# Transposed powers of a chunked scan made on VectorE, and a new order of the second token tile's stages

## Chip, cores and metric

One core of one Trainium2 chip (trn2). The metric is the device time of one execution in microseconds. TensorE's clock has two levels, 1.2 and 2.4 GHz; the profile shows the granted clock as a share of the upper one.

## The reference, cut to what matters

256 tokens of width 1024, all in f32, pass through two blocks. The first mixes the tokens and then retrieves 128 rows for each token out of 16384 (gathered from HBM by index). The second is a hybrid layer with 32 experts:

```
h = rms_norm(x) * (1 + scale1) + shift1
proj = h @ w_in
y_rwkv = rwkv7_time_mix(...)      # per head: state = state * w + (state @ -kk) (kk*a)^T + v k^T
y_moba = moba_attention(...)      # causal attention here, one block of 256 keys
x = x + gate1 * (concat(y_rwkv, y_moba) @ w_out)
h = rms_norm(x) * (1 + scale2) + shift2
x = x + gate2 * moe(h)            # top 4 of 32 experts, each with 12 MB of weights
```

The recurrence of the time mix runs over all 256 tokens, for 8 heads of 64 channels.

## The kernel before

**Two tiles of 128 tokens.** After the first block's mixing, the kernel retrieves 256 picks (128 for each tile): GpSimd gathers a row for each of 128 tokens, VectorE makes the dot products, ScalarE the weights, TensorE the weighted sums. The second block's mixing of the first tile (all of the hybrid layer up to the router) is spread over the retrieval of the second tile's picks; the second tile's mixing follows alone. Then come the 32 experts, each with six 2 MB pairs of weight chunks.

**What sets the order.** Every engine runs the stages of a tile as generators (`attention`, `values`, `mixer`, `output`), which yield a stage's name before it. For the first tile, `first_slots()` gives each name a pick, and an engine runs the stage at that pick (`up_to`; ScalarE one pick ahead, TensorE two). For the second tile, `to_end` always takes the generator whose next stage stands first in the hand-written list `ORDER`. Each engine executes in its order and waits on semaphores; a generator's own order is never changed by the list.

**The scan.** The time mix works in chunks of 32 tokens (`CL`). Per chunk and head, "gram0" and "gram1" are the products of the scaled keys with the scaled queries (L2229, masked by VectorE at L1618). The inverse of a strictly triangular 32x32 matrix is built from powers in five levels: `si[:, :, 0]` holds the power S, `si[:, :, 1]` the inverse so far, and `nts`/`pw_t` in turn the transposed power. Each level has two groups of 32 products, the fifth only one (8 heads by 4 chunks, `within`, L2253; each product gives two matmul and two load records): one makes the next transposed power, which ScalarE copies out of PSUM (L1027), the other the next power and the next term of the inverse, which VectorE copies and adds (L1663, L1665). The first transposed matrix comes from TensorE as "nt" (L2243), masked by VectorE (L1652). Then follow z1 and wu (L2253, L2292: the inverse applied), the chunk products fg (L2310), phi (L1682), the state from chunk to chunk (st: L2336 and L1691), q2 and yp (L2320), ys (L2354) and a group norm (ln2, ln3). "tok0" to "tok3" are four transposed tensors (L2213), "aff" is eight small operations that fold the norm's gain and bias into the gate (L1635, L1640).

**The attention.** mb0 to mb3 are the products for query and key, each in two halves (L2071), mb4 and mb5 those for the values (L2128); msum sums the squares (L2078) that VectorE makes (L1405), mscore the scores (L2090; VectorE L1421 reads them), soft the maxima, exp the exponentials on ScalarE, prob the scaling by VectorE (L1438), mturn the turned probabilities (L2101, copied by ScalarE at L934), att the product with the values (L2111).

**The output projection** is in two parts: om0 to om3 for the attention's half (L2411), or0 to or3 for the scan's half (L2371). Norm, router and the first expert follow.

**The weights' queue.** SyncE issues all loads in order. After the stream of the layer's weights come the experts' pairs into ten places. Pairs 1 to 5 wait for the ring slots of rw, mb and others; the sixth waits for att of the second tile (`pv_mm`), the seventh for yp and fg:

```
elif m == 5:
    sp.wait_ge(pv_mm, TT)
elif m == 6:
    sp.wait_ge(yp_mm, TT)
    sp.wait_ge(fg_mm, 4 * TT)
```

The eighth and ninth wait for or1 and or3 (ring slots of the output projection), the tenth for the router, and each later one for the pair that has been read ten before it.

Of the kernel before, what the change touches and what calls it, by code (L numbers as in the profile page):

```python
# [10 lines left out]
ALU = mybir.AluOpType  # L11
# [47 lines left out]
GRAM_BANK = (2, 0)  # L59
TOK_BANK = {3: 4, 0: 1, 1: 3, 2: 4}  # L60
# [117 lines left out]
def first_slots():  # L178
    at = {"sum": 0, "norm": 1, "gain": 2, "norm1": 3, "xn": 4, "xres": 5, "turn": 6, "msq": 20, "msum": 21, "rms": 22, "qk": 23, "mscore0": 24, "soft0": 26,
# [3 lines left out]
          "tok3": 41, "aff": 42, "gram1": 43, "nt": 44, "tok0": 47, "tok1": 51, "tok2": 55, "z1": 64, "wu": 65, "phi0": 71, "phi1": 72, "q2": 78, "yp": 79,  # L183
# [20 lines left out]
rw5.0 rw5.1 exps mixr kmod rw6.0 rw6.1 rkk rw7.0 bonus rw7.1 mixv gup kk mb0.0 mb0.1 tilde mb1.0 mb1.1 bon gram0 tok3 aff mb2.0 mb2.1 gram1 nt  # L204
mb3.0 mb3.1 msq pow1 tok0 msum rms pow2 tok1 mb4.0 qk pow3 tok2 mscore0 soft0 mb4.1 mscore1 exp0 pow4 soft1 mb5.0 pow5 exp1
mb5.1 prob0 z1 mturn0 prob1 wu mturn1 fg0 fg1 fg2 fg3 att phi0 st0 phi1 om0 st1 om1 st2 q2 yp om2 st3 ys ln2 om3 ln3
# [61 lines left out]
def build(nc, xd, stream, colsd, matsd, rowsd, badad, expert_uv, w_gate_up, w_down, bias_moe, out):  # L268
    with ExitStack() as ctx:
# [261 lines left out]
        nt_mm = sem("nt_mm")  # L531
# [3 lines left out]
        pt_mm = sem("pt_mm")  # L535
# [246 lines left out]
        def _(act):  # L782
# [163 lines left out]
            def mixer(tt):  # L946
# [92 lines left out]
                act.preload_act_table_set("natural_log_exp_and_others")  # L1039
# [74 lines left out]
        def _(dve):  # L1114
# [283 lines left out]
            def attention(tt):  # L1398
# [42 lines left out]
            def mixer(tt):  # L1441
# [180 lines left out]
                grams(0)  # L1622
                yield "tok3"
# [6 lines left out]
                yield "aff"  # L1630

                dve.wait_ge(tilde, tt + 1)
                dve.wait_ge(sig_out, 9 * tt + 9)
                for c in range(4):
                    dve.scalar_tensor_tensor(bon[tt][:, c, :], bon[tt][:, c, :], col("ln_b", c), gg[tt][:, c, :], ALU.add,  # L1635
                                             ALU.mult).then_inc(vec_step, 1)
                steps[0] += 4
                dve.wait_ge(vec_step, steps[0])
                for c in range(4):
                    dve.tensor_scalar(gg[tt][:, c, :], gg[tt][:, c, :], col("ln_g", c), None,  # L1640
                                      ALU.mult).then_inc(vec_step, 1)
                steps[0] += 4
# [993 lines left out]
```

## Time and profile before

| | |
|---|---|
| median of 3 runs | 1935.63 us (1935.39 to 1938.67) |
| the profiled execution | 1940.42 us, span 1938.6 us |
| TensorE, matmuls busy | 1709.2 us, 88% |
| VectorE busy | 918.2 us, 47% |
| ScalarE busy | 471.6 us, 24% |
| GpSimd busy | 285.6 us, 15% |
| HBM read | 770.53 MB, 398 GB/s over the span |
| mean granted clock | 0.942 |

The shares are averages over stages with different limits: mixing of the first block (to about 190 us), retrieval (to about 887 us), the second tile (to about 1016 us) and the experts. The 2 MB pairs of the experts take 28.6 us from issue to landing by the page, because several are on their way at once. A line of the timeline merges successive instructions of one kind, and the idle time in brackets is that before the first of them. "issue" as a releaser means that the engine waited for nothing that the profile shows.

### The profile page before, as it was taken

The page shows a single profiled execution, that of the slowest core. Times are in us where ns is not written, and L with a number is a line of the kernel's source. Part 1 is how long each engine was busy: PE and PEld are TensorE (multiplying, and loading weights), DVE is VectorE, ACT ScalarE, POOL GpSimd, SP SyncE. Part 2 cuts the span into 40 slices and gives each one's busy share as a digit, 9 for nine tenths or more (in the row PEclk, how much of TensorE's full clock was granted, in tenths as well). Part 3 has the DMA queues.
Part 4 walks back from the last instruction along what each step waited for, and adds up shares of the span by engine and source line. Part 5 has one row for each costly group of instructions (what it writes and reads, how often), then busy time and mean ns, then how long its engine had stood idle before and what let it go on. Part 6 is the DMA issues. An engine that isn't in the chain of part 4 may idle for free.

```text
span 1938.6 us, 29728 instructions
## 1 busy us (share of the span) xinstructions
PE 1709.2 (88%) x12010; PEld 801.4 (41%) x12010; DVE 918.2 (47%) x1994; ACT 471.6 (24%) x1191; POOL 285.6 (15%) x286
## 2 busy tenths in 40 slices
PE   9999988666679876879989999999999999999997
PEld 7888554211135533416873333333333333333332
DVE  4755877788664765555532323232323223222222
ACT  1011443433344633443221111011011101111100
POOL 1001433344433243350000000000000000000000
PEclk9999998866679999878999999999999999999999
DMA  9992999999999999999559999999999999999996
GB/s 392 381 410 114 422 420 421 421 421 421 421 421 420 421 419 420 414 414 373 234 219 388 426 427 427 428 428 428 428 428 428 427 428 428 428 428 428 428 428 294
DMA packets 81850, 772.98 MB, mean 399 GB/s; under 512 B 9076, under 2 KB 9332, under 8 KB 10200
## 3 DMA queue, kind: packets, MB, share of 16 engines
q1 hardware_dynamic: 44192, 500.50, 61.5%
q0 software_dynamic: 36864, 268.45, 33.4%
q10 hardware_dynamic: 696, 2.66, 0.4%
q8 instruction: 69, 1.13, 0.2%
q14 instruction: 29, 0.24, 0.0%
HBM read 770.53 MB, written 1.05 MB: 398 GB/s over the span
## 4 chain that ended last, share of the span: by engine, by line
PE 39%; DMA 8%; DVE 4%; issue 2%; ACT 0%; SPq 0%; DVEq 0%; ACTq 0%
PE psum L2476 18%; PE psum L2507 10%; DMA ring<-in_w_gate_up 4%; PE psum L2519 3%; DMA gates_mats<-in_w_gate_up 2%; DMA arena<-in_w_gate_up 2%; PE psum L2172 1%; PE psum L2490 1%; DVE arena L1821 1%; DVE arena L1824 1%; DVE arena L1818 1%; DVE arena L1819 1%; PE psum L2071 1%; PE psum L2462 1%; PE psum L2128 0%
## 5 line engine op out<-in xcount | busy, mean ns | idle before, releaser
L2036 PE MATMUL psum<-ring,arena 64*64 64x512 f32 x1584 | 267.5, 759 | 130.5 <-ACT arena L903 130.1
L1392 DVE CUSTOM_DVE_ANT_0 ring<-ring,arena 128x1024 f32<-128x1024 f32 x198 | 241.7, 1225 | 133.7 <-DMA ring<-in_expert_uv,arena 131.9
L2476 PE MATMUL psum<-ring,arena 128*64 128x512 f32 x1232 | 273.3, 594 | 3.3 <-DMA ring<-in_w_gate_up 3.2
L767 POOL DMA_INDIRECT ring<-in_expert_uv,arena x198 | 211.8, 1070 | 321.4 <-PE psum L2036 299.8
L1818 DVE TENSOR_SCALAR arena<-psum 128x512 f32<-128x512 f32 x32 | 22.1, 692 | 374.3 <-PE psum L2476 374.3
L1102 ACT ACTIVATE arena<-arena 128x512 f32<-128x512 f32 x32 | 20.2, 630 | 732.1 <-DVE arena L1818 732.1
L2036 PEld LDWEIGHTS psum<-ring,arena 64*64 64x64 f32 x1584 | 49.2, 153 | 286.1 <-ACT arena L903 272.3
L2476 PEld LDWEIGHTS psum<-ring,arena 128*64 128x64 f32 x1232 | 86.5, 137 | 183.8 <-issue 174.9
L2476 PE MATMUL psum<-arena 128*64 128x512 f32 x608 | 136.7, 595 | 1.7 <-DMA arena<-in_w_gate_up 0.9
L2507 PE MATMUL psum<-ring,arena 128*64 128x512 f32 x608 | 136.9, 595 | 0.0
L894 ACT ACTIVATE late<-late 128x1 f32<-128x1 f32 x256 | 51.7, 202 | 309.3 <-DVE late L1392 305.8
L1879 PE MATMUL psum<-arena,ring 128*128 128x256 f32 x512 | 111.7, 379 | 0.1
L1827 DVE TENSOR_TENSOR arena<-psum,arena 128x512 f32<-128x512 f32 x32 | 22.1, 692 | 188.4 <-PE psum L2507 188.4
L1879 PEld LDWEIGHTS psum<-arena,ring 128*128 128x128 f32 x512 | 96.9, 190 | 13.7 <-issue 0.4
L767 POOL DMA_INDIRECT arena<-in_expert_uv,arena x58 | 63.6, 1096 | 257.5 <-DVE arena L1355 170.2
L2036 PE MATMUL psum<-arena 64*64 64x512 f32 x464 | 76.0, 735 | 28.0 <-ACT arena L903 27.9
L1830 DVE TENSOR_TENSOR xres<-xres,psum 128x1024 f32<-128x1024 f32 x64 | 75.3, 1218 | 40.8 <-PE psum L2519 40.8
L1392 DVE CUSTOM_DVE_ANT_0 arena<-arena 128x1024 f32<-128x1024 f32 x58 | 70.9, 1225 | 43.6 <-DMA arena<-in_expert_uv,arena 42.9
L903 ACT ACTIVATE arena<-ident,peer_w 128x64 f32<-128x64 f32 x256 | 89.0, 348 | 8.4
L2519 PE MATMUL psum<-arena 64*128 64x512 f32 x256 | 63.6, 611 | 26.9 <-issue 26.9
L2476 PEld LDWEIGHTS psum<-arena 128*64 128x64 f32 x608 | 42.3, 137 | 91.5 <-issue 87.1
L898 ACT ACTIVATE peer_w<-late,peer_g 128x1 f32<-128x1 f32 x256 | 75.4, 294 | 8.9
(381 smaller groups left out, 2038.7 us busy)
## 6 DMA issues: line engine op xcount, KB each, us to landing
ring<-in_w_gate_up SPq DMA_DIRECT2D x77, 2048.0 KB, 28.6
ring<-in_stream SPq DMA_DIRECT2D x91, 1024.0 KB, 11.1
arena<-in_w_gate_up SPq DMA_DIRECT2D x38, 2048.0 KB, 29.2
ring<-in_w_down SPq DMA_DIRECT2D x38, 2048.0 KB, 28.6
arena<-in_w_down SPq DMA_DIRECT2D x20, 2048.0 KB, 28.6
gates_mats<-in_w_gate_up SPq DMA_DIRECT2D x13, 2048.0 KB, 28.1
gates_mats<-in_w_down SPq DMA_DIRECT2D x6, 2048.0 KB, 30.6
ring<-in_expert_uv,arena POOLq DMA_INDIRECT x198, 17.9
```

Of the source, the lines that this page charges most:

```text
L767: pool.indirect_dma_start(rows_of[b].rearrange("p u d -> p (u d)"), None, expert_uv, bass.IndirectOffsetOnAxis(peer_i[:, tt, k:k + 1], 0)) ...
L894: act.activation(one, one, ACT.Gelu).then_inc(weight_step, 1)
L898: act.activation(peer_w[:, 0, c % 4:c % 4 + 1], one, ACT.Copy, scale=peer_g[:, tt, k:k + 1]).then_inc(weight_step, 1)
L903: act.activation(diag[:, c % 4, :], ident2[:], ACT.Copy, scale=peer_w[:, 0, c % 4:c % 4 + 1]).then_inc(diag_ready, 1)
L1392: dve.tensor_tensor_reduce(u, u, h2[tt], 1.0, 0.0, ALU.mult, ALU.add, peer_h[:, tt, k:k + 1]).then_inc(dot_done, 1)
L1818: dve.tensor_scalar(ag, psum[:, 0, :], LIMIT, None, ALU.min).then_inc(gate_ready, 1)
L1830: dve.tensor_tensor(xres[:, tt, :], xres[:, tt, :], psum[:, (6, 3)[tt]:(8, 5)[tt], :].rearrange("p a c -> p (a c)"), ALU.add).then_inc(acc ...
L1879: last = pe.matmul(psum[:, bank, c * T:(c + 1) * T], wide(n)[:, k, c * P:(c + 1) * P], acts[:, k, :], start=(k == 0), stop=(k == KD - 1))
L2036: last = pe.matmul(psum[o:o + 64, 6 * tt + h, :], diag[rows, c % 4, :], rows_of[b][rows, 1, h * 512:(h + 1) * 512], start=(k == 0), stop=( ...
L2476: last = pe.matmul(psum[CAP * h:CAP * h + CAP, gu, :], x, w[:, at:at + 512], start=False, stop=(kt == GU_CHUNKS - 1), skip_group_check=True)
L2507: last = pe.matmul(psum[CAP * h:CAP * h + CAP, 5, :], a_in, w[:, i * D + h * 512:i * D + h * 512 + 512], start=False, stop=(kt == KD - 1), ...
L2519: last = pe.matmul(psum[:, (6, 3)[tt] + h, :], sct[rows, tt, :], ye[rows, :], start=True, stop=True)
```

## The change

- The transposed matrix and the transposed powers come from VectorE, as transposes of 32x32 blocks from SBUF to SBUF (five of 128x256 a tile). "nt" and the four groups of products for transposed powers (levels 1 to 4) go from TensorE, with their copies on ScalarE; level 4 now makes a power and a term at once (64 columns). All powers go to PSUM bank 2.
- tok0, tok1 and tok2 stand after level 3 and level 5, all copied by ScalarE; tok3 stands before gram0 on TensorE.
- "aff" moves from before gram1 to after the first chunk's state.
- "msq" is two stages, each waiting for its own copy.
- `ORDER`: in the second tile the scan's products stand first, the attention's later stages follow the states, and om0 to om3 stand behind ys.
- The second tile drops one load of ScalarE's table at ln2.

```diff
+POW_BANK = 2
...
-    at = {"sum": 0, "norm": 1, "gain": 2, "norm1": 3, "xn": 4, "xres": 5, "turn": 6, "msq": 20, "msum": 21, "rms": 22, "qk": 23, "mscore0": 24, "soft0": 26,
+    at = {"sum": 0, "norm": 1, "gain": 2, "norm1": 3, "xn": 4, "xres": 5, "turn": 6, "msq0": 16, "msq1": 20, "msum": 21, "rms": 22, "qk": 23, "mscore0": 24, "soft0": 26,
-          "tok3": 41, "aff": 42, "gram1": 43, "nt": 44, "tok0": 47, "tok1": 51, "tok2": 55, "z1": 64, "wu": 65, "phi0": 71, "phi1": 72, "q2": 78, "yp": 79,
+          "nt": 41, "tok3": 42, "gram1": 43, "tok0": 55, "tok1": 56, "tok2": 63, "z1": 64, "aff": 75, "wu": 65, "phi0": 71, "phi1": 72, "q2": 78, "yp": 79,
...
-rw5.0 rw5.1 exps mixr kmod rw6.0 rw6.1 rkk rw7.0 bonus rw7.1 mixv gup kk mb0.0 mb0.1 tilde mb1.0 mb1.1 bon gram0 tok3 aff mb2.0 mb2.1 gram1 nt
-mb3.0 mb3.1 msq pow1 tok0 msum rms pow2 tok1 mb4.0 qk pow3 tok2 mscore0 soft0 mb4.1 mscore1 exp0 pow4 soft1 mb5.0 pow5 exp1
-mb5.1 prob0 z1 mturn0 prob1 wu mturn1 fg0 fg1 fg2 fg3 att phi0 st0 phi1 om0 st1 om1 st2 q2 yp om2 st3 ys ln2 om3 ln3
+rw5.0 rw5.1 exps mixr kmod rw6.0 rw6.1 rkk rw7.0 bonus rw7.1 mixv gup kk mb0.0 mb0.1 tilde mb1.0 mb1.1 bon gram0 nt tok3 mb2.0 gram1 pow1 mb2.1 msq0 pow2
+mb3.0 pow3 tok0 tok1 mb3.1 msq1 pow4 msum rms pow5 tok2 mb4.0 z1 qk mb4.1 mscore0 soft0 wu mb5.0 mb5.1 mscore1 exp0 fg0 fg1 soft1 fg2 fg3
+phi0 exp1 phi1 st0 st1 aff st2 q2 prob0 mturn0 prob1 yp mturn1 st3 att ys om0 om1 ln2 om2 om3 ln3
...
-                for lv in range(1, 5):
-                    yield "pow%d" % lv
-                    dst = (nts, pw_t)[lv % 2][tt]
-                    act.wait_ge(pt_mm, 4 * tt + lv)
-                    act.copy(dst, psum[:, 2, 0:T].rearrange("p (h t) -> p h t", h=NH)).then_inc(pt_out, 1)
-                    if lv in (1, 3):
-                        i = lv - 1
-                        yield "tok%d" % i
-                        act.wait_ge(tok_mm, 4 * tt + i + 2)
-                        dst = tok[tt][:, i, :].rearrange("p (h c) -> p h c", h=NH) if i else az[tt][:, :, 0, :]
-                        act.copy(dst, psum[:, TOK_BANK[i], :].rearrange("p (h c) -> p h c", h=NH)).then_inc(tok_ready, 1)
+                for i in range(3):
+                    yield "tok%d" % i
+                    act.wait_ge(tok_mm, 4 * tt + i + 2)
+                    dst = tok[tt][:, i, :].rearrange("p (h c) -> p h c", h=NH) if i else az[tt][:, :, 0, :]
+                    act.copy(dst, psum[:, TOK_BANK[i], :].rearrange("p (h c) -> p h c", h=NH)).then_inc(tok_ready, 1)
...
-                act.preload_act_table_set("natural_log_exp_and_others")
+                if tt == 0:
+                    act.preload_act_table_set("natural_log_exp_and_others")
...
-                yield "msq"
-                dve.wait_ge(mb_out, 3 * tt + 2)
                 for i, src in enumerate((mq[tt], mk[:, :, tt * P:(tt + 1) * P])):
-                    ins = dve.tensor_tensor(msq[tt][:, i, :].rearrange("p (a t) -> p a t", a=4), src, src, ALU.mult)
-                ins.then_inc(msq_ready, 1)
+                    yield "msq%d" % i
+                    dve.wait_ge(mb_out, 3 * tt + i + 1)
+                    dve.tensor_tensor(msq[tt][:, i, :].rearrange("p (a t) -> p a t", a=4), src, src,
+                                      ALU.mult).then_inc(msq_ready, 1)
...
+                yield "nt"
+                dve.wait_ge(gram_out, 2 * tt + 1)
+                dve.transpose(nts[tt], gr[tt][:, 0, :, 0:CL]).then_inc(nt_out, 1)
+                dve.tensor_tensor(si[tt][:, :, 1, :], gr[tt][:, 0, :, 0:CL],
+                                  ident_c[:].unsqueeze(1).to_broadcast([P, NH, CL]), ALU.add).then_inc(nt_out, 1)
...
-                yield "aff"
+                def affine():
...
-                yield "nt"
-                dve.wait_ge(gram_out, 2 * tt + 1)
-                sh = [P, NH, CL]
-                dve.tensor_tensor(si[tt][:, :, 1, :], gr[tt][:, 0, :, 0:CL], ident_c[:].unsqueeze(1).to_broadcast(sh),
-                                  ALU.add).then_inc(nt_out, 1)
-                dve.wait_ge(nt_mm, tt + 1)
-                dve.tensor_tensor(nts[tt].rearrange("p (c b) t -> p b c t", b=2),
-                                  psum[:, 2:4, 0:P].rearrange("p b (c t) -> p b c t", c=4),
-                                  mask_ts[:].unsqueeze(1).unsqueeze(1).to_broadcast([P, 2, 4, CL]),
-                                  ALU.mult).then_inc(nt_out, 1)
 
                 for lv in range(1, 6):
                     yield "pow%d" % lv
                     dve.wait_ge(ps_mm, 5 * tt + lv)
-                    w = 2 * CL if lv in (2, 3) else CL
-                    out = psum[:, 0, 0:NH * w].rearrange("p (h t) -> p h t", h=NH)
-                    if lv < 4:
+                    w = 2 * CL if 1 < lv < 5 else CL
+                    out = psum[:, POW_BANK, 0:NH * w].rearrange("p (h t) -> p h t", h=NH)
+                    if lv < 5:
                         dve.tensor_copy(si[tt][:, :, 0, :], out[:, :, 0:CL]).then_inc(ps_out, 1)
+                        dve.wait_ge(ps_out, 4 * tt + lv)
+                        dve.transpose((nts, pw_t)[lv % 2][tt], si[tt][:, :, 0, :]).then_inc(pt_out, 1)
                     if lv > 1:
                         dve.tensor_tensor(si[tt][:, :, 1, :], si[tt][:, :, 1, :], out[:, :, w - CL:w],
                                           ALU.add).then_inc(ix_out, 1)
-                    if lv == 2:
-                        yield "tok1"
-                        dve.wait_ge(tok_mm, 4 * tt + 3)
-                        dve.tensor_copy(tok[tt][:, 1, :], psum[:, TOK_BANK[1], :]).then_inc(tok_ready, 1)
...
+                    if c == 0:
+                        yield "aff"
+                        affine()
...
+                yield "tok3"
+                pe.wait_ge(ym_ready, 1)
+                pe.wait_ge(tilde, tt + 1)
+                by_token(3, ps[tt][:, 8:12, :])
...
-                yield "nt"
-                pe.wait_ge(gram_out, 2 * tt + 1)
-                for c in range(4):
-                    for ch in range(P // CL):
-                        ts = chunk_rows(ch)
-                        for par in range(2):
-                            rows = slice(HD * par, HD * par + HD)
-                            last = pe.matmul(psum[ts, 2 + par, c * CL:(c + 1) * CL], ar[tt][rows, c, 0, ts], bt[tt][rows, c, ts],
-                                             start=True, stop=True)
-                last.then_inc(nt_mm, 1)
-
                 def within(bank, lhs, rhs, w):
...
-                    s_src = si[tt][:, :, 0, :] if lv > 1 else gr[tt][:, 0, :, 0:CL]
                     t_src = (pw_t, nts)[lv % 2][tt]
                     yield "pow%d" % lv
                     if lv == 1:
                         pe.wait_ge(nt_out, 2 * tt + 2)
-                        pe.wait_ge(gram_out, 2 * tt + 2)
                     else:
                         pe.wait_ge(pt_out, 4 * tt + lv - 1)
-                        pe.wait_ge(ps_out, 3 * tt + min(lv - 1, 3))
-                    if lv < 5:
-                        within(2, s_src, lambda ts, h: t_src[ts, h, :], CL).then_inc(pt_mm, 1)
                     if lv > 2:
                         pe.wait_ge(ix_out, 4 * tt + lv - 2)
-                    within(0, t_src, (begun, both, both, inverse, inverse)[lv - 1],
-                           2 * CL if lv in (2, 3) else CL).then_inc(ps_mm, 1)
-                    if lv < 4:
-                        yield "tok%d" % (lv - 1)
-                        by_token(lv - 1, (ar[tt][:, :, 0, :], bt[tt], kt_[tt])[lv - 1])
+                    within(POW_BANK, t_src, (begun, both, both, both, inverse)[lv - 1],
+                           2 * CL if 1 < lv < 5 else CL).then_inc(ps_mm, 1)
+                    for i in {3: (0, 1), 5: (2,)}.get(lv, ()):
+                        yield "tok%d" % i
+                        pe.wait_ge(gram_out, 2 * tt + 2)
+                        by_token(i, (ar[tt][:, :, 0, :], bt[tt], kt_[tt])[i])
```

## Rows read from the trace of the kernel before

**Rows 1.** Chain of waits: start us, us, what (its part from 1697 us).
```profile
1697.56 39.38 DMA ring<-in_w_gate_up
```

**Rows 2.** Table of stretches; busy us of each engine (instructions), granted clock, DMA share, GB/s.
```profile
400.00:850.00 450.00, 338.18 (x3356) 142.60 (x3356) 298.46 (x653) 196.15 (x599) 182.51 (x169) 0.84 1.01 419
927.90:1003.00 75.10, 66.22 (x1673) 56.62 (x1672) 31.92 (x76) 19.79 (x40) 0.00 (x0) 0.93 0.52 197
952.30:955.70 3.40, 3.40 (x73) 3.06 (x63) 1.35 (x3) 0.37 (x1) 0.00 (x0) 0.50 0.04 14
979.60:986.50 6.90, 6.41 (x98) 5.78 (x99) 1.71 (x3) 0.58 (x1) 0.00 (x0) 0.51 0.19 38
1023.00:1026.20 3.20, 3.20 (x18) 1.15 (x16) 0.51 (x2) 0.00 (x0) 0.00 (x0) 1.00 0.12 51
1029.00:1900.00 871.00, 834.05 (x4120) 291.33 (x4116) 247.67 (x427) 107.14 (x155) 0.00 (x0) 1.00 1.01 428
```

**Rows 3.** Timeline of SP's queue: start us, us, DMA issued (q: queue).
```profile
984.81 0.33 SPq L671 DMA_DIRECT2D arena<-in_w_down  x1
...
1006.79 4.12 SPq L671 DMA_DIRECT2D ring<-in_w_gate_up  x2
...
1026.26 0.33 SPq L671 DMA_DIRECT2D arena<-in_w_down  x1
```

**Rows 4.** Timeline of TensorE: start us, us, line, operation, count [idle before, releaser].
```profile
927.91 7.41 PE L2071 MATMUL psum<-arena,ring 128*128 128x128 f32 x64
...
945.36 1.31 PE L2253 MATMUL psum<-arena 32*32 32x32 f32 x128
...
951.84 2.18 PE L2253 MATMUL psum<-arena 32*32 32x32 f32 x99 [2.05 <-issue]
...
965.81 0.32 PE L2253 MATMUL psum<-arena 32*32 32x32 f32 x13 [1.30 <-issue]
...
970.59 1.10 PE L2253 MATMUL psum<-arena 32*32 32x64 f32 x64
...
980.09 1.07 PE L2310 MATMUL psum<-arena 32*64 32x64 f32 x48 [2.69 <-issue]
...
993.55 1.06 PE L2320 MATMUL psum<-arena 32*64 32x32 f32 x83 [1.11 <-issue]
...
999.54 1.89 PE L2411 MATMUL psum<-ring,arena 128*128 128x256 f32 x8
1003.04 7.17 PE L2371 MATMUL psum<-ring,arena 128*128 128x256 f32 x32 [1.61 <-DVE arena L1711]
```

**Rows 5.** Groups by line, shapes apart, of VectorE, then ScalarE, 927.9 to 1003.04 us.
```profile
L1421 DVE SCALAR_TENSOR_TENSOR arena<-arena,psum 128x256 f32<-128x256 f32 x8 | 2.8, 416 | 0.8 <-PE psum L2090 0.8
...
L1438 DVE TENSOR_SCALAR arena<-arena,gsm 128x256 f32<-128x256 f32 x8 | 2.3, 350 | 0.1
...
L1618 DVE TENSOR_TENSOR arena<-psum,mask_st 128x512 f32<-128x512 f32 x2 | 1.4, 692 | 4.7 <-PE psum L2229 4.7
...
L1663 DVE COPY arena<-psum 128x256 f32<-128x256 f32 x3 | 1.3, 423 | 8.1 <-PE psum L2253 8.1
L1635 DVE SCALAR_TENSOR_TENSOR arena<-arena,cols 128x128 f32<-128x128 f32 x4 | 1.1, 344 | 0.0
L1640 DVE TENSOR_SCALAR arena<-arena,cols 128x128 f32<-128x128 f32 x4 | 0.9, 282 | 0.0
...
L934 ACT COPY arena<-psum 128x1024 f32<-128x1024 f32 x2 | 2.0, 1012 | 3.4 <-PE psum L2101 3.4
...
L914 ACT COPY arena<-psum 128x512 f32<-128x512 f32 x2 | 1.2, 585 | 16.3 <-PE psum L2071 16.3
```

**Rows 6.** DMA view, queues, 927.9 to 1003 us: packets, MB, share.
```profile
q8 instruction: 14, 0.23, 1.3%
```

**Rows 7.** The page, DMA issues: count, us from issue to landing.
```profile
ring<-in_expert_uv,arena POOLq DMA_INDIRECT x198, 17.9
```

More of the change, by code:

```diff
@@ L530, in build @@
         gram_out = sem("gram_out")
-        nt_mm = sem("nt_mm")
         nt_out = sem("nt_out")
@@ L534, in build @@
         ps_out = sem("ps_out")
-        pt_mm = sem("pt_mm")
         pt_out = sem("pt_out")
@@ L1629, in mixer @@
                                          ALU.mult, ALU.add).then_inc(tok_ready, 1)
-                yield "aff"
-                dve.wait_ge(tilde, tt + 1)
-                dve.wait_ge(sig_out, 9 * tt + 9)
-                for c in range(4):
[L1635 to L1642, printed above, removed]
+                def affine():
+                    dve.wait_ge(tilde, tt + 1)
+                    dve.wait_ge(sig_out, 9 * tt + 9)
+                    for c in range(4):
+                        dve.scalar_tensor_tensor(bon[tt][:, c, :], bon[tt][:, c, :], col("ln_b", c), gg[tt][:, c, :],
+                                                 ALU.add, ALU.mult).then_inc(vec_step, 1)
+                    steps[0] += 4
+                    dve.wait_ge(vec_step, steps[0])
+                    for c in range(4):
+                        dve.tensor_scalar(gg[tt][:, c, :], gg[tt][:, c, :], col("ln_g", c), None,
+                                          ALU.mult).then_inc(vec_step, 1)
+                    steps[0] += 4
                 yield "gram1"
                 grams(1)
-                yield "nt"
-                dve.wait_ge(gram_out, 2 * tt + 1)
-                sh = [P, NH, CL]
-                dve.tensor_tensor(si[tt][:, :, 1, :], gr[tt][:, 0, :, 0:CL], ident_c[:].unsqueeze(1).to_broadcast(sh),
-                                  ALU.add).then_inc(nt_out, 1)
-                dve.wait_ge(nt_mm, tt + 1)
-                dve.tensor_tensor(nts[tt].rearrange("p (c b) t -> p b c t", b=2),
-                                  psum[:, 2:4, 0:P].rearrange("p b (c t) -> p b c t", c=4),
-                                  mask_ts[:].unsqueeze(1).unsqueeze(1).to_broadcast([P, 2, 4, CL]),
-                                  ALU.mult).then_inc(nt_out, 1)
                 for lv in range(1, 6):
@@ L2074, in attention @@
                 yield "msum"
-                pe.wait_ge(msq_ready, tt + 1)
+                pe.wait_ge(msq_ready, 2 * tt + 2)
                 pe.wait_ge(mb_out, 3 * tt + 2 if tt else 3)
@@ L2231, in mixer @@
                     last.then_inc(gram_mm, 1)
-                    if i == 0:
-                        yield "tok3"
-                        pe.wait_ge(ym_ready, 1)
-                        by_token(3, ps[tt][:, 8:12, :])
-                yield "nt"
-                pe.wait_ge(gram_out, 2 * tt + 1)
-                for c in range(4):
-                    for ch in range(P // CL):
-                        ts = chunk_rows(ch)
-                        for par in range(2):
-                            rows = slice(HD * par, HD * par + HD)
-                            last = pe.matmul(psum[ts, 2 + par, c * CL:(c + 1) * CL], ar[tt][rows, c, 0, ts], bt[tt][rows, c, ts],
-                                             start=True, stop=True)
-                last.then_inc(nt_mm, 1)
                 def within(bank, lhs, rhs, w):
```

## The prediction, made blind

> **What bounds the kernel now.** I read the end of the chain of waits first. From 1697 us to the end it is made of waits for expert weights, the first of them 39.4 us long [rows 1]: the end is set by the transfers, not by the arithmetic. The table of stretches says since when: from 1029 to 1900 us the DMA share is 1.01 at 428 GB/s [rows 2]. Just before, from 1023 to 1026.2 us, the share is 0.12 [rows 2]: nothing was on its way. The queue's timeline tells why: ten 2 MB pairs are prefetched, the eighth and ninth of them issued from 1006.79 on, and the eleventh goes out only at 1026.26 [rows 3], when TensorE has read the first pair. From there 182 pairs remain, 381.7 MB, at 428 GB/s 892 us, so the last lands near 1919, and one expert's rest brings the span to 1938.6. **Every microsecond by which TensorE reaches the first expert earlier moves the end by one**, as long as the prefetched pairs have landed by then. Before that, the first tile's mixing is spread over the retrieval of the second tile's rows, where the DMA share is 1.01 at 419 GB/s while VectorE is busy for 298 and TensorE for 338 of 450 us [rows 2]. What is saved there is saved beside a full DMA. So the change counts in the second tile's stretch alone.
>
> **The stretch.** TensorE's timeline: the second tile's attention products begin at 927.91 and the output projection at 1003.04 [rows 4], 75.1 us, of which the rest up to 1026.26 (23.2 us) is untouched. Four idle times in it have the releaser "issue": 2.05, 1.30, 2.69 and 1.11 us [rows 4]; one, 1.6 us, waits for VectorE ahead of the projection [rows 4]. With 0.2 us elsewhere that is 8.9 us idle. Two stretches run at a granted clock of 0.50 and 0.51: 3.4 and 6.9 us [rows 2], 9.8 us of busy time at 1.2 instead of 2.4 GHz, which cost about half, 4.9 us. The work at full clock is 75.1 - 8.9 - 4.9 = **61.3 us**.
>
> **The change, part by part, in that stretch.**
> - *Products removed.* The 32-product matrix "nt" and the transposed product of levels 1 to 4 go, five calls of 64 matmul records. Two calls took 1.31 us in level 1 [rows 4], so 0.65 each: -3.3 us. Level 4 now writes 64 columns instead of 32: a 64-column call took 1.10 us [rows 4], so +0.3. New work: 61.3 - 3.3 + 0.3 = **58.3 us**.
> - *VectorE's five transposes*, 128x256 each, have no row. Below they are bounded by the same size read and written in SBUF, 0.35 us (0.28 from start to start), above by twice the elements, 0.69 us; I take the copy of the same size, 0.42 [rows 5], the nearest row. The Trainium skill ("VectorE: DVE Perf Modes", The three transpose paths) gives 311 ns for 128x128 in bf16; an estimate from it, with 128 more columns at 0.96 GHz, is 0.44 us, and the sum would be the same by it. Per level VectorE then does copy, transpose and sum, 0.42 + 0.42 + 0.42 = about 1.3 us with hand-overs. TensorE has meanwhile one half-chunk of the attention, 7.41 / 4 = 1.85 us [rows 4]. So levels 2 and 3 start about 0.5 us after their operands are there, level 4 after 1.7, level 5 after 0.8: the chain of powers is hidden, by the half-chunks; at 0.69 us for a transpose they are just hidden still. If that cover were gone, it would be 1.3 us a level, 5 us. The five ScalarE copies that they replace (0.37 each) and the 0.69 us copy of "tok1", now ScalarE's, are off the path.
> - *The scan first, attention last.* This makes new waits for TensorE, which I walk through with the durations of before. (a) msum behind ScalarE's copy 0.58 and VectorE's square 0.69 [rows 5] of the key half, while level 4 covers 0.96: 0.5 us. (b) The first scores behind z1's copy and the scaling, 0.69 + 1.4, with mb4.1 (1.9) beside: 0.3. (c) After the chunk products, VectorE still has the second scores (four operations of 0.42 [rows 5], overlapping to 1.4), their maxima (two reductions over 512 columns of 0.69 and two small operations, 1.6) and phi0 (0.69): 1.4. (d) The first state behind phi1 and its own 0.42: 0.5. (e) The second state behind "aff", which VectorE now does there, four of 0.34 and four of 0.28 us [rows 5], 2.0 us: 1.8. (f) The turned probabilities behind the third state's 0.42 and prob0, 1.35, with q2 (0.7) beside: 1.2. (g) Attention's last products behind ScalarE's copy of 1.01 us [rows 5]: 1.1. Sum **6.9 us**. The 1.6 us ahead of the output projection go: from the start of om3 at 999.54 to or0 at 1003.04 ScalarE and VectorE need 3.5 us, of which om3 covers 1.9 [rows 4]; now om2 and om3 stand there and cover 3.8. So the table load (1.28 us) that the second tile drops is worth nothing by itself.
> - *The queue.* SP waits in order, and its sixth pair, issued at 984.81 [rows 3], waits for the attention's last product, the seventh for yp. In the new order yp comes first and both pairs go out together, at the attention's last product. That is four om pieces, 7.6 us, and more before or0. Two pairs need 10 us of DMA at 428 GB/s; the eighth is due 3.8 us after or0 starts (1006.79 [rows 3]), so at least 11.4 us later, and the tenth had landed 3 us before the first was read. The transfers start later and end in time: 0. If the attention came over 4 us later still, this would turn into a loss.
> - *Idle "issue" times.* They fall in dense runs of small products, and the queue of instructions moved 14 packets in this stretch [rows 6], for 1673 matmul and 1672 load records [rows 2]: I take them for waits on instruction fetch. The change takes out 640 of the instructions, all in the powers, where 3.3 of the 7.1 us lie; 3.8 lie in the chunk products and yp, which stay as dense. Bounds 0 and 7.1; taken: 2.7.
> - *Clock.* The halved stretches followed the idle times of 2.05 and 2.69 us; no idle time of up to 1.6 us was followed by one. The new waits (c) to (f) are 4.9 us within some 8, with a stall before them, so one halved stretch as long as the longer one before, 6.9 us, is likely, part of it over waits. Bounds 0 and 4.9 us; taken: 2.8.
> - *The first tile.* The same edits. VectorE's gram0 now comes two places before TensorE's (tok3 stands first there at slot 42), which holds the dots up once by some 4 us. A gathered row lands 17.9 us after its issue [rows 7], and 1.05 MB at 419 GB/s take 2.5 us, so seven are on their way and the DMA stays covered: 0, at most 1 us.
>
> **Sum.** 58.3 + 6.9 + 2.7 + 2.8 = 70.7 us against 75.1: **-4.4 us**. The profiled execution took 1940.4 us (span 1938.6 and 1.8 around it) and would take 1936.0; it lies 4.8 above the median of the runs, 1935.63. On that median the change gives **1931.2 us**.
>
> **Rivals.**
> 1. *Nothing is lost on the way.* Stalls 0.5 and clock 0.5: 66.2 us, -8.9, so 1926.7. For it: every new idle time is single and below 1.8 us. Against: they come in a row, and the chunk products are the place of the longest stall.
> 2. *The new waits eat the gain.* The idle "issue" times stay at 7.1 us because the fetch, not the number of products, sets the pace, clock cost 2.8: 75.1 us, no change, 1935.6; with the clock at 4.9 it is 1937.7. For it: the scan's small products now stand closer together, with one half-chunk between levels instead of two or three pieces. Against: half as many instructions a level.
> 3. *Slower: the clock is halved in the output projection.* Place: om0 to or3. Four om pieces of 1.9 and or's 7.2 us [rows 4], 14.8 us, were interleaved or ran at full clock, and now stand behind the cluster of waits. If all of it ran at 1.2 GHz, it would take 14.8 us more: 58.3 + 6.9 + 2.7 + 14.8 = 82.7, +7.6 us, 1943.2. It turns the sign once the halved work exceeds 7.2 us at full clock. Against: the projection is dense, and before, the pieces of om and or that came behind idle times of 1.1 and 1.6 us ran at full clock. The Trainium skill ("TensorE: Matmul & The Clock Gate", HAM oscillation — how this bites in real kernels) says that repeated waits of TensorE between short groups of products return it to half rate every time. The trace agrees in its two halved stretches.
> 4. *The change does nothing where it counts*, because transfers set the end anyway. Against it stands the idle DMA before 1026 us [rows 2], so I give it nothing of its own.
>
> **How the numbers follow.** A measurement of this kernel tells some 0.2%, 3.9 us, from no change. Forecast 0.47, rival 1 0.16, rival 2 0.27, rival 3 0.10. My forecast lies just beyond the 0.2%, so about a fifth of its chance falls into "same". Faster 0.37 + 0.16 = 0.53; same 0.10 + 0.22 = 0.32 with what is left of rival 2 (0.05) slower, and rival 3 slower: 0.15. The range runs from rival 1 (1926.7) to just beyond rival 2 with a short clock loss, 1936.7; it leaves out the slow cases.
>
> **What would show it.** Right: the eleventh pair issued near 1022, DMA share 1.01 from there on; TensorE's gaps (c) to (f) around 970 to 977; the sixth and seventh pair issued together near 985; transposes of 0.35 to 0.5 us; no ScalarE copy at the powers. Wrong: a transpose above 0.7 us, DMA still busy when the first pair has been read, idle "issue" times above 5 us in the stretch, a granted clock of 0.5 in om or or, or a second tile that starts its attention at another time than 928 us, which would mean that the first tile's part counts.

## The result, and the profile after

The changed kernel took **1945.38 us** in the median of ten runs (1941.07 to 1950.13). The kernel before, run on the same chip, took 1937.87 (ten runs, 1935.03 to 1942.92). The ratio is 1.0034, 95% interval 1.0022 to 1.0045: **slower by about 6.6 us** by the ratio, 7.5 by the medians, where 4.4 us less were forecast. The profiled execution took 1947.6 us, span 1945.8 (before: 1940.42 and 1938.6). The ten runs lie in two groups, four of 1941.1 to 1943.3 us with a mean granted clock of 0.936 to 0.941 and six of 1945.3 to 1950.1 us with 0.924 to 0.932, and the profiled one is of the second.

First the queue's timeline of the changed kernel, as [rows 3] (start us, us, engine, line, operation, count; idle time in brackets before it):

```profile
969.85 0.33 SPq L670 DMA_DIRECT2D ring<-in_w_down  x1
996.77 0.33 SPq L670 DMA_DIRECT2D arena<-in_w_down  x1
997.20 0.38 SPq L670 DMA_DIRECT2D arena<-in_w_gate_up  x1
1010.40 4.13 SPq L670 DMA_DIRECT2D ring<-in_w_gate_up  x2
1018.82 0.33 SPq L670 DMA_DIRECT2D gates_mats<-in_w_gate_up  x1
1033.78 0.33 SPq L670 DMA_DIRECT2D arena<-in_w_down  x1
```

The eleventh pair goes out at 1033.78 instead of 1026.26. From there to the end of the span it is 912.0 us, before 912.3: the whole loss lies ahead of the eleventh pair, which goes out 7.5 us later, and the end follows it one to one. Next the table of stretches (window: length, then busy us of PE, PEld, DVE, ACT and POOL with instructions; granted clock, DMA share, GB/s), as [rows 2]:

```profile
928.70:1006.80 78.10, 66.22 (x1354) 57.69 (x1354) 33.12 (x80) 17.73 (x36) 0.00 (x0) 0.85 0.46 178
946.00:949.40 3.40, 3.40 (x28) 3.24 (x17) 1.18 (x3) 0.00 (x0) 0.00 (x0) 0.50 0.02 5
976.70:997.20 20.50, 15.19 (x329) 13.32 (x331) 7.60 (x25) 2.44 (x3) 0.00 (x0) 0.50 0.01 4
1006.80:1033.60 26.80, 25.37 (x115) 15.12 (x115) 10.44 (x33) 5.19 (x8) 0.00 (x0) 0.81 0.69 274
1017.70:1027.90 10.20, 10.20 (x35) 4.28 (x35) 3.29 (x19) 2.23 (x4) 0.00 (x0) 0.50 0.93 393
986.10:991.95 5.85, 5.85 (x144) 5.05 (x144) 1.93 (x7) 1.01 (x1) 0.00 (x0) 0.50 0.01 3
997.30:1013.80 16.50, 16.50 (x128) 14.71 (x125) 3.86 (x8) 3.79 (x8) 0.00 (x0) 1.00 0.87 324
```

The stretch grew from 75.1 to 78.1 us although 319 matmul records left it. For 20.5 us on end, from the chunk products to the end of the attention, TensorE has the lower clock, 1.2 GHz; and 10.2 us behind the stretch have it too. The last two windows are used further down: one lies within the 20.5 us and holds no idle time at all, the other holds the whole output projection. TensorE's timeline, as [rows 4], shows what lies in and before the 20.5 us:

```profile
945.15 1.12 PE L2231 MATMUL psum<-arena 32*32 32x64 f32 x58 [2.11 <-issue]
970.81 2.01 PE L2284 MATMUL psum<-arena 32*64 32x64 f32 x161
977.53 0.73 PE L2284 MATMUL psum<-arena 32*64 32x64 f32 x31 [4.71 <-issue]
979.18 1.12 PE L2310 MATMUL psum<-gates_mats,arena 64*64 64x64 f32 x16 [0.92 <-DVE arena L1668]
980.92 1.12 PE L2310 MATMUL psum<-gates_mats,arena 64*64 64x64 f32 x16 [0.62 <-DVE gates_mats L1677]
983.21 1.12 PE L2310 MATMUL psum<-arena 64*64 64x64 f32 x16 [1.17 <-DVE arena L1677]
986.10 1.97 PE L2090 MATMUL psum<-ident,arena 128*128 128x128 f32 x8 [0.67 <-DVE arena L1432]
993.05 3.68 PE L2100 MATMUL psum<-arena 128*64 128x128 f32 x32 [1.10 <-ACT arena L933]
```

The idle times with a named releaser shown here are the forecast's (c) to (g), and mostly shorter than forecast: 0.92 (1.4), 0.62 (0.5), 1.17 (1.8), 0.67 (1.2), 1.10 (1.1). The one with the releaser "issue" in the chunk products is 4.71 us. VectorE's transposes, by its groups:

```profile
L1653 DVE STREAM_TRANSPOSE arena<-arena 128x256 f32<-128x256 f32 x4 | 1.8, 446 | 0.1
```

**The sum beside the forecast.** Idle 78.1 - 66.2 = 11.9 us, of which "issue" 2.11 + 4.71 = 6.8 and other waits 5.1. Busy at half clock 3.4 + 15.2 = 18.6 us, half of it lost, 9.3 (7.6 of it in the 20.5 us). The rest is work at full clock: 66.2 - 9.3 = 56.9.

| us | forecast | measured |
|---|---|---|
| work at full clock | 58.3 | 56.9 |
| new waits | 6.9 | 5.1 |
| idle, "issue" | 2.7 | 6.8 |
| clock | 2.8 | 9.3 |
| stretch | 70.7 | 78.1 |
| rest to the eleventh pair | 23.2 | 27.0 |
| start of the stretch | 927.9 | 928.7 |

### The profile page after: what moved, and what is told of

Its sections match the earlier page's. It is cut to its first block, busy times and chain, and to the rows that moved or that the text cites. A ratio compares the mean times of both kernels' runs of the same rounds, so it can differ in the third digit from the quotient of the medians.

```text
span 1945.8 us, 28447 instructions
## 1 busy us (share of the span) xinstructions
PE 1717.8 (88%) x11370; PEld 808.8 (42%) x11370; DVE 920.7 (47%) x2002; ACT 468.6 (24%) x1184; POOL 291.5 (15%) x286
## 4 chain that ended last, share of the span: by engine, by line
PE 41%; DMA 6%; DVE 5%; issue 2%; ACT 0%; SPq 0%; DVEq 0%; ACTq 0%
PE psum L2450 19%; PE psum L2481 11%; PE psum L2493 3%; DMA gates_mats<-in_w_gate_up 2%; DMA ring<-in_w_gate_up 2%; DMA arena<-in_w_gate_up 2%; PE psum L2161 1%; PE psum L2464 1%; DVE arena L1810 1%; DVE arena L1813 1%; DVE arena L1807 1%; DVE arena L1808 1%; PE psum L2060 1%; PE psum L2436 1%; PE psum L2385 0%
## 5 line engine op out<-in xcount | busy, mean ns | idle before, releaser
L766 POOL DMA_INDIRECT ring<-in_expert_uv,arena x198 | 219.3, 1108 | 321.1 <-PE psum L2025 295.9
```

The lines of the kernel that those rows point to most:

```text
L766: pool.indirect_dma_start(rows_of[b].rearrange("p u d -> p (u d)"), None, expert_uv, bass.IndirectOffsetOnAxis(peer_i[:, tt, k:k + 1], 0)) ...
```

## The experiments

Every kernel computes everything. The first two runs and e5 add single things to the changed kernel. e3 and e4 take apart what the change joined: the transposes on VectorE, and the second tile's order. The medians of before that stand behind the ratios were taken beside each group of runs (1938.2 to 1939.2 us).

**e1: fillers.** Products whose result nobody reads, ahead of the states and the attention's late stages:

```diff
+                    if tt and par == 0:
+                        idle_products(1, 3, 2)
...
+                if tt:
+                    idle_products(2, 3, 2)
...
+                    if tt and ch < 3:
+                        idle_products((2, 1, 2)[ch], 0, 2)
```

> The changed kernel with idle TensorE products (128x256, about 0.6 us each at full clock) added in the second tile where it waited: two ahead of the first state, one ahead of the second, two ahead of the third, one ahead of the turned probabilities, two ahead of the attention's last products. Theory 'clock': the changed kernel loses its time at the halved clock (20.5 us from 976.7 us on and 10.2 us from 1017.7 on), which the waits (c) to (g) keep up. Then the halved stretch shrinks to 10 us or less and the kernel comes 4 to 6 us below the changed one, level with before or better. Rival 'stall': the one idle time of 4.7 us ahead of the waits sets the clock by itself and the fillers are too late: the same halved stretch, and the fillers cost up to 3 us more, as they run at the half rate.

Measured: 1943.07 us, ratio to before 1.0019 (1.0008 to 1.003), 2.3 us less than the changed kernel, where 4 to 6 were expected. The execution that the profile shows took 1940.13 us, the least of e1's eleven. Windows of it, the second being its only stretch of half clock behind the chunk products:

```profile
928.70:1001.10 72.40, 64.10 (x1371) 54.27 (x1370) 33.17 (x80) 17.73 (x36) 0.00 (x0) 0.98 0.50 195
975.60:979.00 3.40, 3.27 (x47) 2.33 (x49) 1.29 (x2) 0.00 (x0) 0.00 (x0) 0.50 0.03 10
1001.10:1024.10 23.00, 21.17 (x115) 13.38 (x115) 10.44 (x33) 5.19 (x8) 0.00 (x0) 1.00 0.84 327
```

20.5 us of half clock became 3.4, and the 10.2 us behind the stretch are gone as well (clock 1.00). The 4.4 us of "issue" before it stayed, so the long idle time alone doesn't keep the clock at half. Of the nine profiles with the new order in whole or in part, the three with fillers (e1, e5, e12) have 0 to 3.4 us of half clock behind the start of the chunk products, the six without have 13.6 to 20.5. But the fillers do two things: they close the waits, and they put large products (128 rows, 256 columns) between the scan's small ones. In the changed kernel's window 986.10 to 991.95 TensorE is busy all the time, and the clock is still at half. No run tells the two apart.

**e2: the fifth pair later.** SP holds it until the chunk products have run:

```diff
+                    if m == 4:
+                        sp.wait_ge(fg_mm, 4 * TT)
```

> The changed kernel, whose queue holds back the fifth expert pair (issued at 969.85 us in the changed kernel's profile) until the chunk products are done. Theory 'fetch behind weights': the idle 'issue' time of 4.7 us in the chunk products comes from an instruction packet that waits behind this pair's 2 MB on the DMA engines; with the pair held back it falls to 1.5 us or less, the clock falls later or for less long, and the kernel is 4 to 8 us faster than the changed one. The pair still lands in time, since the DMA is idle otherwise. Rival 'fetch pace': the packets come no faster than TensorE asks for them, whatever else the DMA does; the idle time stays at 3 to 5 us and the total within 2 us of the changed kernel.

Measured: 1943.17 us, 1.0018 (1.0007 to 1.003), 2.2 us less than the changed kernel, where 4 to 8 were expected. The profiled execution of e2 took 1938.02 us, the least of its eleven, so the profiles differ by more than the medians do. The reason shows in the packets of the two kernels. In the changed kernel, from 970.8 to 975 us, only the pair's weights move:

```profile
DMA packets 90, 1.47 MB, mean 351 GB/s; under 512 B 0, under 2 KB 0, under 8 KB 0
q1 hardware_dynamic: 90, 1.47, 100.4%
```

The next 1.5 us bring one packet of instructions:

```profile
q8 instruction: 1, 0.02, 4.1%
```

It comes at 975.12, 4.3 us after the chunk products began (970.81), and TensorE goes on 2.4 us later, at 977.53. In e2, TensorE's timeline, then the queue's, then the window at half clock:

```profile
968.94 2.01 PE L2286 MATMUL psum<-arena 32*64 32x64 f32 x161
972.35 0.49 PE L2286 MATMUL psum<-arena 32*64 32x64 f32 x31 [1.40 <-issue]
```

```profile
973.07 0.33 SPq L670 DMA_DIRECT2D ring<-in_w_down  x1
```

```profile
974.10:991.20 17.10, 13.54 (x289) 11.84 (x286) 6.53 (x24) 2.29 (x5) 0.00 (x0) 0.50 0.31 118
```

The same 161 records run, the same 31 follow. The packet came at 970.00, 1.1 us after the chunk products began, and TensorE again went on 2.4 us later, at 972.35. The packet's 3.2 us of delay are the 3.3 us by which the idle time is longer. **The fifth pair, which mb5.1 releases, kept back a packet of instructions that TensorE needed at once.** The other profiles agree. Where the pair goes out about 1 us ahead of the chunk products (the changed kernel, e1, e4, e6, e11), the packet comes 4.2 to 4.5 us after their start and the idle time is 4.4 to 4.7 us. Where the pair is held back (e2, e5, e8, e12), it comes after 1.0 to 1.2 us and the idle time is 1.4 to 1.8 us. In all 14 profiles TensorE goes on 2.2 to 2.6 us after the packet.

The half clock lasts 17.1 us in e2, though no idle time of its stretch behind the start of the chunk products is longer than 1.40 us. (The intervals of e1 and e2 each overlap with the changed kernel's; e5 is clear of it.)

**e5: both.**

> The changed kernel with both edits at once: the idle TensorE products of e1_fill in its waits and the fifth expert pair held back as in e2_late5. Each alone took 2.3 us off the changed kernel's median. If the clock and the stall are the whole loss against the forecast (4.7 us of idle time and some 20 us at the halved clock), both together bring the kernel to 1938 or below. If they only hide each other, it stays at 1941 to 1943, and what is left is the new order's own: waits in a row with nothing beside them.

Measured: 1939.29 us, 0.9999 (0.9986 to 1.0012): 6.1 us less than the changed kernel, level with before. 1938 or less was expected if clock and idle time were the whole loss. Stretch 71.7 us, idle "issue" 4.1, half clock 6.8, all of it ahead of the chunk products.

**e3 and e4 take the change apart.** e3 has the transposes, the small moves of stages that go with them and the first tile's new slots, but the order of before in the second tile:

```diff
+... bon gram0 nt tok3 mb2.0 mb2.1 gram1
+mb3.0 mb3.1 msq0 msq1 pow1 msum rms pow2 mb4.0 qk pow3 tok0 tok1 mscore0 soft0 mb4.1 mscore1 exp0 pow4 soft1 mb5.0 pow5 tok2 exp1
+mb5.1 prob0 z1 mturn0 prob1 wu mturn1 fg0 fg1 fg2 fg3 att phi0 st0 phi1 om0 aff st1 om1 st2 q2 yp om2 st3 ys ln2 om3 ln3
```

> The changed kernel with the second tile's stages in the order of before (attention between the levels, om pieces between the states), so the transposes on VectorE without the new order. If the new order costs the time (waits in a row, clock), this is faster than before by the removed products, 2 to 5 us, and 8 to 12 us below the changed kernel. If the transposes cost it (VectorE's chain per level longer than the ScalarE copy), this is as slow as the changed kernel or slower.

Measured: **1935.01 us, 0.998 (0.9971 to 0.999): 3.2 us faster than before.** The stretch of e3, and its two idle times in TensorE's timeline:

```profile
930.40:998.10 67.70, 61.75 (x1353) 52.39 (x1352) 33.15 (x80) 17.43 (x36) 0.00 (x0) 0.95 0.57 212
```

```profile
975.14 1.06 PE L2284 MATMUL psum<-arena 32*64 32x64 f32 x48 [2.24 <-issue]
988.28 1.34 PE L2294 MATMUL psum<-arena 32*64 32x32 f32 x82 [2.01 <-issue]
```

The stretch is 7.4 us shorter than before, but began 2.5 later (the first tile's part, below), and the profiled run of before lay 2.2 above its own median here.

e4 is the kernel before, with its products for the transposed powers, in the new order:

```diff
+... bon gram0 tok3 aff mb2.0 gram1 nt mb2.1 pow1 tok0
+mb3.0 pow2 tok1 mb3.1 msq pow3 tok2 msum rms pow4 mb4.0 pow5 z1 qk mb4.1 mscore0 soft0 wu mb5.0 mb5.1 mscore1 exp0 fg0 fg1 soft1 fg2 fg3
+phi0 exp1 phi1 st0 st1 st2 q2 prob0 mturn0 prob1 yp mturn1 st3 att ys om0 om1 ln2 om2 om3 ln3
```

> The kernel before, with the new order of the second tile's stages and its own TensorE products for the transposed powers; 'aff' stays where it was. If the new order costs the time, this is 5 to 10 us slower than before and at least level with the changed kernel, since it also keeps the dense small products with their idle 'issue' times. If the transposes cost it, it is within 3 us of before.

Measured: 1949.85 us, 1.0046 (1.0027 to 1.0064); its eight runs spread from 1942.35 to 1953.65. By the medians against before: transposes alone -3.2 us, order alone +11.6, both +7.5. **The order costs 10.7 to 11.6 us, the transposes save 3.2 to 4.1.** The 3.2 is clear of noise; the 4.1 is not, since the intervals of e4 and of the changed kernel overlap. By the ratios the order costs 9 to 10.5 us.

**e6 and e7 halve the order.** e6 keeps the new order up to fg3 and goes on with the attention first, as before; e7 is e3 up to mb5.1, then the scan first, the attention's late stages and om at the end:

```diff
+exp1 prob0 mturn0 prob1 mturn1 att phi0 st0 phi1 om0 aff st1 om1 st2 q2 yp om2 st3 ys ln2 om3 ln3
...
+mb5.1 z1 wu fg0 fg1 fg2 fg3
+phi0 phi1 st0 st1 aff st2 q2 prob0 mturn0 prob1 yp mturn1 st3 att ys om0 om1 ln2 om2 om3 ln3
```

> The changed kernel with the new order only up to the chunk products: the levels of the scan stand early, but the attention is finished ahead of the states, and the om pieces stand between the states as before. Theory 'second half': the loss of the new order (10.4 us between e3_oldorder's median and the changed kernel's) lies behind the chunk products, in the waits for aff, prob and mturn, the clock they bring down and the om pieces no longer beside the states; then this is within 2 us of e3_oldorder's 1935. Theory 'dense first half': the close-set small products cost it; then this is 5 us or more above e3_oldorder.

> The counterpart: the order of before up to wu, the new one from the chunk products on (states in a row with aff, the attention's turned probabilities and its last products behind them, om at the end). Theory 'second half': 7 us or more above e3_oldorder's 1935, near the changed kernel's 1945. Theory 'dense first half': within 3 us of e3_oldorder.

Measured: e6 1946.80 us (1.0037, 1.0026 to 1.0049), e7 1943.18 (1.002, 1.0009 to 1.0032), against e3's 1935.01. Neither theory came true, since both halves cost: 11.8 and 8.2 us, which don't add up. e6 has the long "issue" idle time, 8.8 us of "issue" in all, and 13.6 us of half clock behind it; e7 has the long half clock without the long idle time. TensorE's timeline of e6, then of e7 with a window of its table of stretches:

```profile
977.86 0.73 PE L2284 MATMUL psum<-arena 32*64 32x64 f32 x31 [4.68 <-issue]
```

```profile
974.20 0.73 PE L2285 MATMUL psum<-arena 32*64 32x64 f32 x31 [2.68 <-issue]
975.85 1.12 PE L2311 MATMUL psum<-gates_mats,arena 64*64 64x64 f32 x16 [0.91 <-DVE arena L1669]
989.73 3.68 PE L2101 MATMUL psum<-arena 128*64 128x128 f32 x32 [1.10 <-ACT arena L934]
```

```profile
974.20:993.20 19.00, 14.52 (x319) 12.78 (x319) 7.60 (x25) 2.02 (x2) 0.00 (x0) 0.50 0.01 3
```

In e7 the fifth pair went out at 964.81, 4.6 us ahead of the chunk products instead of 1.0, the packet came between 971.5 and 972, and the idle time is 2.68 instead of 4.71 us. The half clock lasted 20.5 us, from 974.1 to 994.6, as long as in the changed kernel. Before, where the idle time was the same (2.69), 6.9 us of half clock followed; what differs behind it is the order.

**e8: e3 with e2's wait.**

> e3_oldorder (transposes on VectorE, old order) with the fifth expert pair held back until the chunk products are done. If an instruction packet waits behind that pair, the idle 'issue' time of 2.2 us in the chunk products falls below 1, the clock dip behind it goes, and the median falls by 1 to 3 us from 1935. If the packets' pace is their own, no change.

Measured: 1935.20 us, 0.9978 (0.9966 to 0.999), the same as e3; the expected gain did not come. TensorE's timeline shows why, beside e3's two idle times above:

```profile
972.28 0.92 PE L2286 MATMUL psum<-arena 32*64 32x64 f32 x48 [1.42 <-issue]
987.01 1.48 PE L2296 MATMUL psum<-arena 32*64 32x32 f32 x82 [3.31 <-issue]
```

The first idle time did fall, from 2.24 to 1.42: in e3 the pair, sent at 965.80, kept the DMA busy until 972.5, and the packet came at 972.77, 1.8 us after the chunk products began (971.01); in e8 it came 1.0 us after. But the held-back pair and the sixth, sent at 973.30 and 976.59, then kept the DMA busy until 984.6, through the start of q2 and yp (982.37). The packet for those came at 984.59, and the idle time there grew from 2.01 to 3.31. The wait moved the delay to the next dense run.

**e9: e3 with long products inside the dense runs.**

```diff
-... fg0 fg1 fg2 fg3 att ... st2 q2 yp om2 st3 ...
+... fg0 fg1 att fg2 fg3 ... st2 q2 om2 yp st3 ...
```

> e3_oldorder (transposes on VectorE, order of before) with long products set into its two dense runs of small ones: the attention's last products between the second and third quarter of the chunk products, and om2 between q2 and yp. Its idle 'issue' times of 2.2 us (chunk products) and 2.0 us (q2 and yp) come there. Theory 'fetch': instructions are used up faster than they arrive only where small products stand close, so spreading takes most of the 4.2 us away and the median falls by 2 to 4 us below 1935. Rival: the attention's last products now release the sixth pair while the chunk products still run, its 2 MB delay the next instruction packet, and the idle time stays or grows; then the median stays at 1935 or rises.

Measured: **1930.97 us, 0.996 (0.9948 to 0.9973)**, ahead of both kernels and, with intervals that just overlap, of e3. Its timeline and stretch:

```profile
970.40 1.33 PE L2284 MATMUL psum<-arena 32*64 32x64 f32 x96
971.66 1.97 PE L2100 MATMUL psum<-arena 128*64 128x128 f32 x32
973.55 0.37 PE L2284 MATMUL psum<-arena 32*64 32x64 f32 x16
974.62 1.11 PE L2284 MATMUL psum<-arena 32*64 32x64 f32 x80 [0.70 <-issue]
```

```profile
929.80:995.20 65.40, 62.00 (x1353) 52.83 (x1353) 33.18 (x80) 17.76 (x36) 0.00 (x0) 0.95 0.60 227
```

With the attention's product between the second and third group of chunk products, and om2 ahead of yp, "issue" fell from 4.2 us in e3 to 0.7. Waits for VectorE of 0.84 and 0.85 us are new, and 6.8 us of half clock are left, at the stretch's end. The attention's product takes 1.97 us here, at full clock, and 3.68 in the changed kernel.

**e10: e9 with the sixth pair held back** until the chunk products have run.

> e9_spread, with the sixth pair held back until the chunk products are done. If its 2 MB delay the instruction packet in e9_spread, this has an idle time in the chunk products under 1 us and is 1 to 3 us faster than e9_spread; if not, the two are equal within 1 us.

Measured: 1931.63 us, 0.9962 (0.9948 to 0.9976), no different from e9. The idle time is 0.43 instead of 0.70 us; there was little left for a pair to lengthen.

**e11: "aff" early.** This is the changed kernel with "aff" between pow5 and tok2 in the list, ahead of z1 on VectorE and out of the states' way; in the first tile it moves from pick 75 to 63.

> The changed kernel with 'aff' (2.0 us on VectorE) between level 5 and z1, where VectorE stood idle, instead of between the first two states. The wait ahead of the third state (1.17 us) and part of the next go. If aff's place is a real part of the loss, 1 to 4 us below the changed kernel's 1945.4 (the wait itself and a shorter stretch at the halved clock). If the waits only move to the next releaser (the turned probabilities), within 1 us of it.

Measured: 1946.34 us, 1.0038 (1.0025 to 1.0052): no gain. Of the waits 0.6 us went (4.5 against 5.1), and the half clock of 20.5 us stayed.

**e12: e11 with e1's fillers and e2's wait**, the best made of the new order.

> The changed kernel with all three: idle products in its waits, the fifth pair held back, aff in VectorE's idle time. If these three are what stands between the changed kernel and the forecast, it falls below e5_fill_late5's 1939.3 by 1 to 2 us, and its stretch from the second tile's attention to the output projection comes to about 71 us. If the new order has a cost of its own, it stays above e3_oldorder's 1935.

Measured: 1938.39 us, 0.9997 (0.9988 to 1.0006). Its stretch is the forecast's sum, 70.7 us:

```profile
929.60:1000.30 70.70, 65.48 (x1369) 55.73 (x1369) 33.21 (x80) 17.73 (x36) 0.00 (x0) 0.95 0.49 191
```

It is 0.9 us below e5, which the noise does not tell from nothing. Even so it is 3.4 us behind e3, whose order has neither filler nor extra wait.

## Why the prediction was wrong

**What held.** The end follows the eleventh pair, and the DMA was idle ahead of it. The transposes took 0.446 us (taken 0.42), and the powers are hidden. The Trainium skill's page "VectorE: DVE Perf Modes", The three transpose paths, has no figure for f32; the trace agrees with the estimate of 0.44 that was worked out from it. The sixth and seventh pair went out together and landed in time. The walk through the new waits was near: 5.1 us for 6.9 (its seven parts as printed add up to 6.8). The work came to 56.9 for 58.3. Of the five copies on ScalarE that were said to go there were four, since VectorE made the first one; that changes no term.

**The step "Clock" failed first.** It reasoned that one stretch of 6.9 us was likely, because single idle times of up to 1.6 us had not been followed by one before. Measured were 3.4 and 20.5 us, cost 9.3 us for 2.8. The 20.5 us cover waits of 0.6 to 1.2 us in a row, between groups of products of 0.7 to 5.9 us. e7 shows that the order lengthens it: with an idle time as long as before's, the half clock lasted 20.5 us instead of 6.9. e2 shows 17.1 us of it with no idle time above 1.40 behind the chunk products' start. e1, e5 and e12 show that large products put between bring it down to 3.4 us or nothing, in e1 with the long idle time still ahead.

What in the order does it is open. The waits are one reading. The other is the kind of work. The scan's products and the turned probabilities ran 5.85 us at half clock without any idle time, and still the clock did not come back. In the changed kernel, e2, e4, e6, e7 and e11 the half clock ended within 1.3 us of the end of the attention's last products (att). They start 22 us behind the start of the chunk products in the changed kernel; in the kernel before they stood right behind the chunk products, and the half clock was short. The Trainium skill ("TensorE: Matmul & The Clock Gate", A second HAM failure mode: psum-queue depth-cycling) describes a kernel in which very short idle times between groups of products are frequent enough that the clock falls and recovers again and again; the trace agrees that idle times of about 1 us can go with the lower clock, but here it stayed down in one piece. The section of the Trainium skill that the prediction cites, HAM oscillation, tells of groups of products of about 2 us, each followed by a wait for the DMA that is longer than the group. The idle time of 4.71 us behind 2.01 us of chunk products is like that; the waits behind it are 0.62 to 1.17 us.

**"Idle issue times" failed second**: 6.8 us for 2.7. The step counted instructions and left the place of the run out. Fewer products did shorten these times where the order stayed: 7.2 to 4.2 us in e3. But the new order puts mb5.1 right ahead of the chunk products, and with it the fifth pair's 2 MB. **"The queue" looked at the sixth and seventh pair and asked only whether they land in time, at a cost of 0**; it did not ask what a pair, the fifth above all, takes the DMA away from. It is 3.3 us, by e2 (4.71 to 1.40).

**"The rest up to 1026.26 is untouched" failed third**: 27.0 us for 23.2. Of this 10.2 us ran at 1.2 GHz, which by half would be 5.1 us lost. Rival 3 had named the lower clock in the output projection, with 1943.2 us. That this is near the measured time is luck: the projection, 998.88 to 1013.8, ran at full clock, and the half clock came behind it, at 1017.7, in the router and the first expert's products. Such a stretch, 6.8 to 10.2 us, stands in the profiles of the changed kernel, e4, e6, e7 and e11, all with 13.6 us or more of half clock between the chunk products and the projection, and or0 at 1003.77 or later. In e1, e5 and e12 it is gone with the long stretch; in e2, which has 17.1 us of it but reaches or0 at 1000.92, it is gone too. What brings it about was not tried, so its cause stays open.

**The first tile** cost about 1 us, the bound of its step: the stretch starts at 928.06 to 930.42 in the twelve profiles with the new slots (mean 929.0), and at 927.91 and 927.85 in the two without, which are few.

Added up: -4.4 forecast, +6.5 clock, +4.1 "issue", -1.8 waits, -1.4 work, +3.8 rest, +0.8 start give +7.6, against 7.5 us at the eleventh pair and 7.2 us in the spans. These are of two single executions, and the changed kernel's lies 2.2 us above its median. The forecast time also stood on a median of three runs, 1935.63, which came to 1937.87 with ten: 2.2 of the 14.2 us between 1931.2 and 1945.38 are that. Rival 2 had the direction (stalls eat the gain) but not the size; the range ended at 1936.7 since it let only one of the three costs go wrong at a time.

## What to carry to other kernels

A list of waits isn't priced by its sum alone: a row of small products with short waits between them can also hold TensorE at half clock, and here that cost 7.6 us beside 4.5 us of waits. Long products are worth most between such groups, as fillers of real work (e9), not gathered at the end. When a stage is moved, ask of every transfer that it releases not only when it must have landed but also what else needs the DMA while it runs, the engine's own instructions among it. Holding a transfer back can move the delay to the next dense run (e8).

## What the runs showed that was not expected

- TensorE's instructions come by DMA, and in dense runs of small products it waits for them: 0.70 us (e9), 1.40 (e2), 2.24 (e3) and 4.71 us (changed kernel) within the same 192 records of chunk products, by what stands between them and what is on its way.
- In the changed kernel the half clock came back 20 us after it had ended (997.2 to 1017.7), 2.3 us behind a single idle time of 0.68 us.
- Work without use may make a kernel faster: the fillers' 2.3 us (e1) and, with the fifth pair held back, 3.9 us (e5 beside e2) point the same way, though each by itself is not clear of noise.
